# Order of the causal attention's units: head after head instead of two heads side by side

## The reference, cut to what matters

```python
for blk in range(s // Q_BLOCK):
    q0, kend = blk * Q_BLOCK, (blk + 1) * Q_BLOCK
    sc = (jnp.einsum('bqhd,bkhd->bhqk', q_nope[:, q0:kend], k_nope[:, :kend])
          + jnp.einsum('bqhd,bkd->bhqk', q_rope[:, q0:kend], k_rope[:, :kend]))
    ...
    pr = jax.nn.softmax(sc, axis=-1).astype(v.dtype)
    outs.append(jnp.einsum('bhqk,bkhd->bqhd', pr, v[:, :kend]))
```

## Time and profile before

| | |
|---|---|
| median of 3 executions | 4122.95 us (4122.6 to 4123.36) |
| profiled execution, its own time | 4122.6 us |
| its span in the profile | 4120.8 us |
| mean granted TensorE clock | 0.952 of full |
| TensorE busy | 3687.2 us, 89% |
| VectorE busy | 2180.2 us, 53% |
| ScalarE busy | 1549.7 us, 38% |
| GpSimd busy | 710.3 us, 17% |

### The profile page before, as it was taken

One profiled execution on the slowest core, in us unless ns is written; L12 is line 12 of the kernel. 1 busy time (PEld: TensorE's weight loads), 2 busy tenths in 40 slices (PEclk: granted clock), 3 DMA queues, 4 the chain that ended last, 5 costly groups with the idle time before them and its releaser, 6 DMA issues.

```text
span 4120.8 us, 46110 instructions
## 1 busy us (share of the span) xinstructions
PE 3687.2 (89%) x18491; PEld 2961.0 (72%) x18491; DVE 2180.2 (53%) x2886; ACT 1549.7 (38%) x1925; POOL 710.3 (17%) x325
## 2 busy tenths in 40 slices
PE   7999997999989989999998787888869599999995
PEld 5566665666667768888885566666647599999995
DVE  3333334535247454554325523434553599999985
ACT  3343432224221232112224422232342477777765
POOL 2010101012112322222222111111102012222210
PEclk9999998999999999999999998998989699999997
DMA  3111113133354224444211131121513499999995
GB/s 116 36 57 47 56 42 109 41 113 113 127 187 173 67 92 138 148 143 149 95 44 44 47 135 48 57 96 52 180 45 136 186 344 380 375 383 383 381 369 203
DMA packets 126101, 611.66 MB, mean 148 GB/s; under 512 B 14217, under 2 KB 15633, under 8 KB 101058
## 3 DMA queue, kind: packets, MB, share of 16 engines
q1 hardware_dynamic: 121138, 591.41, 38.7%
q0 software_dynamic: 4608, 16.78, 1.5%
q10 hardware_dynamic: 144, 0.52, 0.0%
HBM read 525.35 MB, written 83.27 MB: 148 GB/s over the span
## 4 chain that ended last, share of the span: by engine, by line
PE 76%; DVE 12%; ACT 5%; DMA 3%; issue 3%; POOL 1%; SPq 0%; ACTq 0%; DVEq 0%; POOLq 0%
PE bank L263 16%; PE bank L264 15%; PE bank L265 15%; PE bank L2883 4%; PE bank L2882 4%; PE bank L2881 4%; PE bank L2891 2%; PE bank L2893 2%; PE bank L2892 2%; PE bank L592 2%; DVE st L752 1%; PE bank L568 1%; PE bank L550 1%; PE bank L581 1%; DVE stg L1518 1%
## 5 line engine op out<-in xcount | busy, mean ns | idle before, releaser
L263 PE MATMUL bank<-XH,WH 128*128 128x512 f32 (+1 forms) x2696 | 1115.6, 414 | 153.1 <-DVE stg L1812 19.8
L264 PE MATMUL bank<-XL,WH 128*128 128x512 f32 (+1 forms) x2696 | 1068.1, 396 | 0.0
L265 PE MATMUL bank<-XH,WL 128*128 128x512 f32 (+1 forms) x2696 | 1066.0, 395 | 0.0
L251 POOL TENSOR_TENSOR WL<-WR,WH 128x1024 fp32r<-128x1024 f32 (+1 forms) x249 | 492.2, 1977 | 2428.9 <-ACT WH L243 2428.9
L263 PEld LDWEIGHTS bank<-XH,WH 128*128 128x128 f32 x2696 | 518.4, 192 | 338.9 <-issue 86.1
L265 PEld LDWEIGHTS bank<-XH,WL 128*128 128x128 f32 x2696 | 517.9, 192 | 119.6
L264 PEld LDWEIGHTS bank<-XL,WH 128*128 128x128 f32 x2696 | 520.0, 193 | 116.0 <-issue 8.2
L243 ACT ACTIVATE WH<-WR 128x1024 fp32r<-128x1024 f32 (+1 forms) x249 | 216.6, 870 | 640.3 <-PE bank L265 631.1
L2814 DVE TENSOR_TENSOR EL<-ER,EH 128x2816 fp32r<-128x2816 f32 x120 | 369.2, 3082 | 1.7 <-ACT EH L2809 1.7
L2809 ACT ACTIVATE EH<-ER 128x2816 fp32r<-128x2816 f32 x120 | 306.4, 2562 | 149.2 <-PE bank L2883 87.6
L2881 PE MATMUL bank<-EH,WH 128*128 128x352 f32 x1024 | 335.4, 328 | 6.3 <-DVE EL L2814 6.3
(11 more groups left out here) (471 smaller groups left out, 5153.9 us busy)
## 6 DMA issues: line engine op xcount, KB each, us to landing
ER<-in_wu_dram SPq DMA_DIRECT2D x48, 1408.0 KB, 8.7
ER<-in_wd_dram SPq DMA_DIRECT2D x40, 1408.0 KB, 9.8
aq<-in_w_ada_dram SPq DMA_DIRECT2D x96, 512.0 KB, 3.8
WR<-in_w_in_dram SPq DMA_DIRECT2D x89, 512.0 KB, 4.4
ER<-in_wg_dram SPq DMA_DIRECT2D x32, 1408.0 KB, 8.3
res<-in_wg_dram SPq DMA_DIRECT2D x16, 1408.0 KB, 8.2
res<-in_wu_dram SPq DMA_DIRECT2D x16, 1408.0 KB, 8.3
WR<-in_wg_dram SPq DMA_DIRECT2D x16, 1408.0 KB, 8.3
```

What stands on the lines that cost most here:

```text
L251: e.tensor_tensor(WL[:, n % 2 * 1024:n % 2 * 1024 + m], raw, hi.bitcast(F32), ALU.subtract).then_inc(*w_lo.up("w_lo", n))
L263: e.matmul(bank[bk][:, 0:b - a], whi, xhi, start=k == 0, stop=False)
L264: e.matmul(bank[bk][:, 0:b - a], whi, xlo, start=False, stop=False)
L265: mm = e.matmul(bank[bk][:, 0:b - a], wlo, xhi, start=False, stop=k == K - 1)
```

## The change

Four things go together:

- `UNITS` is turned: head 0 with its 8 query blocks, then head 1 with its 8.
- P times V runs after query blocks 3 and 7 of each head, for four query blocks of that head: 512 columns for each key block (fewer near the diagonal), all on the same half of the bank's partitions. `PT` is laid out accordingly, and the waits for `PT`, `B_O` and `yt` are renamed to (a, half of the queries).
- The copy into `yt` takes 64 partitions x 512 columns instead of 128 x 256.
- The main fill becomes `(2, 1, 2, 2, 5, 5, 5, 6)[qb]`, and "mid" and "last" go.

```diff
     q_, k_ = [qk[:, a * T:(a + 1) * T] for a in range(2)], [qk[:, (2 + a) * T:(3 + a) * T] for a in range(2)]
     SEGS = ((cq, 384, "q_norm"), (ckv, 256, "kv_norm"))
     PROJ = ((q_, uq, 384, 3, cq), (k_, ukv, 256, 2, ckv))
-
-    UNITS = [(a, qb) for qb in range(8) for a in range(2)]
+    UNITS = [(a, qb) for a in range(2) for qb in range(8)]
     mla_pe, mla_act, mla_dve = sem("pe_mla"), sem("act_mla"), sem("dve_mla")
     d_mla = [dma_sem(f"mla{i}") for i in range(4)]
     d_dt, d_y = dma_sem("dt_out"), [dma_sem(f"y_out{i}") for i in range(4)]
@@ -503,7 +502,7 @@
             st.upto("mla.proj", i)
             for u in range(16):
                 st.upto("mla.unit", i, u)
-            e.wait_ge(*on("mla.o", i, 3))
+            e.wait_ge(*on("mla.o", i, 1, 1))
             e.dma_start(D_y[i], yt).then_inc(*d_y[0].up("y", i))
 
     def attention_pe(e, st):
@@ -556,12 +555,10 @@
                 a, qb = UNITS[u]
                 if u + 1 < 16:
                     attention_scores_pe(e, i, u + 1)
-                st.fill((2, 2, 2, 2, 4, 4, 4, 5)[qb], "mla.unit", i, u)
+                st.fill((2, 1, 2, 2, 5, 5, 5, 6)[qb], "mla.unit", i, u)
                 p = Pm[:, u % 2 * T:u % 2 * T + T]
                 for k0 in range(0, qb + 1, 4):
                     kn = min(4, qb + 1 - k0)
-                    if k0:
-                        st.fill(1, "mla.mid", i, u)
                     e.wait_ge(*on("mla.p", i, u))
                     e.wait_ge(*on.bank(B_T, "mla.pt", i, u, k0))
                     for k in range(k0, k0 + kn):
@@ -569,19 +566,16 @@
                                          p[:, k * 128:k * 128 + 128], ident)
                     mm.then_inc(*mla_pe.up("mla.tr", i, u, k0))
                 on.at["mla.tr", i, u] = on.at["mla.tr", i, u, k0]
-                if u % 4 == 3:
-                    qp = u // 4
-                    st.fill(2, "mla.last", i, u)
+                if qb % 4 == 3:
+                    qh, hh = qb // 4, 2 * i + a
                     e.wait_ge(*on("mla.pt", i, u, k0))
-                    e.wait_ge(*on.bank(B_O, "mla.o", i, qp))
+                    e.wait_ge(*on.bank(B_O, "mla.o", i, a, qh))
                     for k in range(qb + 1):
-                        o = 128 if k == qb else 0
-                        for a in range(2):
-                            c0, hh = a * 2048 + k * 256, 2 * i + a
-                            mm = e.matmul(bank[B_O][a * 64:a * 64 + 64, qp % 2 * 256 + o:qp % 2 * 256 + 256],
-                                          vN[:, k * 512 + hh * 64:k * 512 + hh * 64 + 64], PT[:, c0 + o:c0 + 256],
-                                          start=k == 0, stop=k == qb)
-                    mm.then_inc(*mla_pe.up("mla.pv", i, qp))
+                        o = max(0, (k - 4 * qh) * 128)
+                        mm = e.matmul(bank[B_O][a * 64:a * 64 + 64, o:512],
+                                      vN[:, k * 512 + hh * 64:k * 512 + hh * 64 + 64],
+                                      PT[:, k * 512 + o:k * 512 + 512], start=k == 0, stop=k == qb)
+                    mm.then_inc(*mla_pe.up("mla.pv", i, a, qh))
 
     def attention_scores_pe(e, i, u):
         a, qb = UNITS[u]
@@ -637,14 +631,13 @@
                 if u + 1 < 16:
                     attention_exp_act(e, i, u + 1)
                 st.upto("mla.unit", i, u)
-                ql = qb % 2
+                ql = qb % 4
                 for k0 in range(0, qb + 1, 4):
                     kn = min(4, qb + 1 - k0)
                     e.wait_ge(*on("mla.tr", i, u, k0))
-                    if u % 4 == 0 and (i or u):
-                        e.wait_ge(*(on("mla.pv", i, u // 4 - 1) if u else on("mla.pv", i - 1, 3)))
-                    e.activation(PT[:, a * 2048:a * 2048 + 2048].rearrange("p (k q) -> p k q", k=8)[
-                                     :, k0:k0 + kn, ql * 128:ql * 128 + 128],
+                    if ql == 0 and (i or u):
+                        e.wait_ge(*on("mla.pv", i if u else i - 1, *((a, 0) if qb else (1 - a, 1))))
+                    e.activation(PT[:, :].rearrange("p (k q) -> p k q", k=8)[:, k0:k0 + kn, ql * 128:ql * 128 + 128],
                                  bank[B_T][:, 0:kn * 128].rearrange("p (k q) -> p k q", q=128), AF.Copy).then_inc(
                         *mla_act.up("mla.pt", i, u, k0))
 
@@ -732,13 +725,13 @@
                 p = Pm[:, u % 2 * T:u % 2 * T + (qb + 1) * 128]
                 e.tensor_scalar(p, p, mst[:, c4 + 5:c4 + 6], None, ALU.mult).then_inc(*V.up("mla.p", i, u))
                 st.upto("mla.unit", i, u)
-                if u % 4 == 3:
-                    qp = u // 4
+                if qb % 4 == 3:
+                    qh = qb // 4
                     if i:
                         e.wait_ge(*on("y", i - 1))
-                    e.wait_ge(*on("mla.pv", i, qp))
-                    e.tensor_copy(yt[:, qp * 256:qp * 256 + 256],
-                                  bank[B_O][:, qp % 2 * 256:qp % 2 * 256 + 256]).then_inc(*V.up("mla.o", i, qp))
+                    e.wait_ge(*on("mla.pv", i, a, qh))
+                    e.tensor_copy(yt[a * 64:a * 64 + 64, half(qh)], bank[B_O][a * 64:a * 64 + 64, :]).then_inc(
+                        *V.up("mla.o", i, a, qh))
 
     def attention_max_dve(e, i, u):
         V = mla_dve
```

## The result

The changed kernel takes 4193.97 us in the median of 4 executions (4186.8 to 4197.8), the kernel before 4123.15 us (4122.6 to 4133.99): ratio **1.0164**, 95% interval 1.0141 to 1.0185. Forecast were 4166 us and at most 4188. The direction was right, the size wrong (+70.8 us in the medians where +43 was forecast), and the time lies outside the range. The profiled execution took 4190.62 us, 68.0 more than that of before.

What follows compares the result with a forecast made beforehand. TensorE, busy 89% of the span, was taken to bound the kernel. Attention +38, pool +13 and SSD -8 gave +43 us on 4122.6, so 4166 us; its own range 4150 to 4182, the full range 4134 to 4188.

Steps and rivals of the forecast that it cites:

- P times V: Attention: one head per group runs at 1.71 instead of 0.85 ns per column, +7.35 us a pass.
- Rival (a): Attention: P times V with two heads apart still runs at 0.85 ns per column; 4137 us, chance 0.09.
- The lost covers: Attention: waits open where fills went or shrank, +9.2 us a pass.
- the term for VectorE: Attention: first transposes wait for VectorE, +1.6 us a pass in small units, -0.6 in large ones.
- the steps that left: Attention: a pass asks for 64 instead of 74 projection steps, -7.0 us a pass, spent elsewhere.
- part 3: Attention: price of removed or shortened fills, from waits on ScalarE's copies and on VectorE, +9.2 us a pass.
- rival (b): Attention: the array pays more on one half, or the clock falls; 4180 to 4190 us, chance 0.10.
- LRU within 2 us: LRU stage: its time may move by 2 us either way.
- SSD -8 and pool +13: Later stages: SSD gains 8 us (between 0 and -14); pool loses 13 us as leftover steps run there.
- the wall at the scan: SSD's start: TensorE waits for VectorE's half-tile copy behind the scan, 8.2 us instead of 13.8.
- the empty pool stage: Pool: the projection ran dry after three steps; now 43 are left, spent as 16, 16 and 11, +13 us.
- The same code takes the same time: First branch matmul to the end, code the change doesn't touch: forecast difference 0.

Runs made afterwards that it cites:

- e2: The changed kernel with the fills of the kernel before (74 steps a pass, mid and last fills back); ratio to before 1.0106.
- e1: The kernel before with P times V doing all of head 0, then all of head 1, instead of alternating; ratio to before 1.0064.
- e3: The kernel before with only the fills of the changed kernel (64 steps a pass, no mid or last fills); ratio to before 1.0056.
- e9: The changed kernel with 8 more projection steps before the first attention pass; one time, 4175.2 us.
- e4: The changed kernel with 4 more projection steps before the first attention pass; ratio to before 1.0138.
- e10: The changed kernel with 12 more projection steps before the first attention pass; one time, 4191.9 us.
- e6: The kernel before with 2 instead of 10 projection steps at the end of SSD; ratio to before 1.0031.
- e5: The kernel before with 24 of the 48 projection steps at LRU's end moved into the pool stage, before its four products; ratio 0.9956.

## Why the prediction was wrong

By its own parts:

- **P times V** (forecast +29 for the four passes): right. 64.2 us at full clock against 33.5, +31 (e2), and the cause, neighbours on different halves of the columns, is shown by e1. Rival (a) is out.
- **The lost covers** (+37): right in kind, too high in size. With the clock taken out e3 gives 27.4 us. By kind of wait, e3 against before: the transposes' waits for copies +20.2 (forecast 19.2), P times V's 12.3 (13.6), the waits for VectorE +1.0 (4.0), 33.5 in all. So the term for VectorE was the most mis-sized. Why the attention pays less than these waits sum to isn't shown. With P times V (30.7), the covers (27.4), the order (3.4) and the steps that left (-28.0) the attention comes to +33.5; e9 shows +32.1, where I had +38.
- **Where the steps fall in the attention**: this is the step that failed. I read single long scales of P in the trace as noise and took the price of a unit from the clean ones. So part 3 prices the second unit of a head at 0.94 us. At 64 steps a pass the split hits that unit of head 1, which has a single step of cover, in every pass, and it waits 2.06. And rival (b) had the clock right, and what I held against it was wrong: I wrote that open waits stay at about a microsecond, while some are 2 us. Both together are 463.4 - 450.0 = 13.4 us, at most 8.5 of them the clock's. That the place of the split decides how much the clock costs is borne out by e4, e9 and e10 in amount, by one profile each; what brings each single fall stays open.
- **LRU within 2 us**: failed for the same reason, +6.8 (4.0 in waits, the rest mostly half clock), shown by e6. I gave no reason for the 2 us.
- **SSD -8 and pool +13**: -7.8 and +14.3. The step count, the wall at the scan and the empty pool stage were read rightly. That SSD's number fits so well is partly luck: its parts are -6.3 at the front, +0.5 in the convolutions, where a load that goes early was to give about 6, and -2.0 in the rest; and the stage differs by 3 us between the two profiles of the kernel before.
- **The same code takes the same time**: not within 9 us. It wasn't in the sum at all, and over the twelve profiles this code spreads by 16 us; whether the change has a part in the 9 stays open.

-6 + 13.4 + 6.8 + 9.1, and 1.3 for the pool stage, make 24.6 of the missing 25 us (68 against 43). What the moved steps drag along, 13.4 and 6.8 us, is the largest part, and nothing in the sum or the range stood for it. Without the 9.1 us of the stages that the change doesn't touch, for which the range had no term either, the profiled execution would still have been at 4181.5 us, inside the range: it took both to leave it.

## What to carry to other kernels

Filler work isn't only time on one engine: here each 16 steps bring a split on GpSimd and copies, and the split slowed the VectorE instructions that ran beside it. Count where they fall, and beware of a period that divides the loop's. Before giving up a pair of matmuls that alternates between halves of the array, read its pace from start to start: it may be running at twice the pace of anything that replaces it. And move filler to where the engine stands anyway (e5), not away from where it covers a wait.

## What the runs showed of the hardware that I had not expected

- The granted clock falls from 2.4 to 1.2 GHz in a stage in which TensorE is busy for 86% and no wait is longer than 2.1 us: seven times in e10, never in e9, with the same instructions. Which waits bring a fall stays open: in e2 a single wait of 1.91 us stood ahead of one, and in the kernel before a wait of 1.93 us brought none.
- VectorE's tensor_scalar beside a GpSimd instruction takes 1.46 us instead of 0.35 (256 values) and 2.70 instead of 0.81 (1024 values) when the GpSimd instruction has started first: it ends 0.15 and 0.55 us behind it. Started 0.6 us ahead of a split, one of 1024 values kept its 0.75 us. Three scalar_tensor_tensor of 1024 values take 5.95 us beside a split instead of 3.93.
- The stages from the first branch matmul to the end, 2970 us of the same code, differ by up to 16 us between profiles, and TensorE's busy time in it by as much (2660 to 2678 us), while that of VectorE and ScalarE stays.
